# Attention step of a two-block kernel: the weighted sum in two groups a step, and one group of maxima moved by one turn

## The chip, the cores and the metric

The kernel runs on one core of one Trainium2 chip. The metric is the device time of one execution in microseconds (us). A core has five engines that run side by side and meet through semaphores: TensorE (PE in the profile, its weight loads PEld), VectorE (DVE), ScalarE (ACT), GpSimd (POOL) and the queue that issues transfers (SP).

## The reference

Two blocks follow each other: a chunked gated linear attention block, and a block with grouped-query attention beside a convolution. The change touches only the attention of the second block:

```python
# 8 query heads of 64, 2 key/value heads, 2048 queries, 256 context keys + 2048 keys = 2304 keys
s = jnp.einsum('bqkgd,bskd->bkgqs', qblk, k).astype(jnp.float32) * scale
pr = jax.nn.softmax(s, axis=-1).astype(v.dtype)
return jnp.einsum('bkgqs,bskd->bqkgd', pr, v)
```

## The kernel before, in words

The program has phases one after another: modulation, the first block, the projections, `attention`, `output`. `attention` walks over 32 steps (8 query heads times 4 blocks of 512 queries). In a step the 2304 keys are 18 tiles of 128, and each key tile is a turn `kt`, 0 to 17. A score tile (L1864, L1865) is two matmuls into one of three PSUM banks `bank_s`; ScalarE turns it into `p_f` by an exponential (L1928).

The exponential needs the negated maximum of each query's row. It is found a step ahead: for step i+1, 20 "pieces" (L1824), matmuls of 128 queries by 512 keys (every fifth by 256), go into four PSUM banks `bank_m`. VectorE reduces each to a column of maxima (L1960), then makes one column of the five (L1965) and negates it into `mz` (L1969). TensorE turns `mz` into a row with four transposes (`max_row`, L1831), and ScalarE copies the row (L1911) into the operand of the next step's scores. The pieces go in five groups of four, at the turns that `PIECES_OF_TURN` marks (2, 4, 9, 10, 14). `max_row(i+1)` stands at turn 15 and waits for `mz`. An even piece p waits until the pieces up to p-3 of its step have been reduced, because it and its neighbour take over banks that those held:

```python
if p % 2 == 0:
    need(pe, mx_read, i * NP + max(p - MBANKS + 2, 0))
```

The weighted sum `p_f` times `v` (L1839) is taken for pairs of key tiles, nine pairs a step, into one bank `bank_o` (`weigh`). `GROUP_AT` says at which turn which pairs stand: pairs 0 to 2 at turn 9, pairs 3 to 5 at turn 14, and pairs 6 to 8 at turn 2 of the next step. Within a turn TensorE's order is: the scores, the pieces of that turn, then the weighted sum of that turn.

The denominators are sums of `p_f` over the key tiles: GpSimd adds pairs 1 to 6 (L1809), VectorE adds pairs 7 and 8 (L1977) and folds (L1981). TensorE sums over partitions (`sum_den`, L1847, turn 5) and spreads the reciprocal (L1854, turn 7); VectorE adds and scales the output (L1985, L1990, L1996). Each engine executes its list strictly in the order written, and a wait at the head holds all that is behind it.

Of the kernel before, what the change touches and what calls it, by code (L numbers as in the profile page):

```python
# [1673 lines left out]
def attention(nc, d, keep):  # L1674
# [5 lines left out]
    POOL_ADDS = 6  # L1680
    DVE_ADDS = NPR - 1 - POOL_ADDS + 1
    SBANKS, MBANKS = 3, 4
    GROUP_AT = {2: (6, 7, 8), 9: (0, 1, 2), 14: (3, 4, 5)}
    GROUP_STEPS = (NQH // NKV) * NB
    STEPS = NKV * GROUP_STEPS
    PIECES = [(qt, n) for qt in range(NT) for n in range(-(-KEYS // TB))]
    NP = len(PIECES)

    PIECES_OF_TURN = [0, 0, 4, 0, 4, 0, 0, 0, 0, 4, 4, 0, 0, 0, 4, 0, 0, 0]
    TURN_PIECES = [list(range(sum(PIECES_OF_TURN[:kt]), sum(PIECES_OF_TURN[:kt + 1]))) for kt in range(NKT)]  # L1690
    assert sum(PIECES_OF_TURN) == NP
    with ExitStack() as ctx:
# [34 lines left out]
        def need(eng, semaphore, n):  # L1727

            if isinstance(n, int) and n <= 0:
                return  # L1730
            eng.wait_ge(semaphore, UP + n)
# [4 lines left out]
        def steps(eng, body):  # L1736


            last = GROUP_STEPS - 1
            for g in range(NKV):  # L1740
                base = g * GROUP_STEPS
                body(base, 0, g, g - 1 if g else None, g)
                body(base + 1, 1, g, g, g)
                with eng.Fori(1, GROUP_STEPS // 2 - 1) as it:
                    for s in range(2):
                        body(it * 2 + (base + s), s, g, g, g)
                body(base + last - 1, 0, g, g, g)
                body(base + last, 1, g, g, g + 1 if g + 1 < NKV else None)

        nc.all_engine_barrier()  # L1750
        with nc.Block() as block:
# [61 lines left out]
            def _(pe):  # L1813
                def piece(i, s, g, p):

                    qt, n = PIECES[p]
                    width = min(TB, KEYS - TB * n)
                    rows = slice(HD * (p % 2), HD * (p % 2 + 1))
                    if p == 0:
                        pe.wait_ge(q_hi_done, UP + i + 1)  # L1820
                        need(pe, row_read, i)
                    if p % 2 == 0:
                        need(pe, mx_read, i * NP + max(p - MBANKS + 2, 0))
                    pe.matmul(M[p % MBANKS][:, 0:width], q_c[s][rows, P * qt:P * (qt + 1)], k_a[g][rows, TB * n:TB * n + width],  # L1824
                              start=True, stop=True).then_inc(mx_done, 1)

                def max_row(i):

                    pe.wait_ge(mz_done, UP + i + 1)
                    for qt in range(NT):  # L1830
                        last = pe.transpose(M[0][0:HD + 1, P * qt:P * (qt + 1)], mz[:, qt, :], ident[:])  # L1831
                    last.then_inc(row_done, 1)

                def weigh(i, s, g, j):
                    pe.wait_ge(p_done, UP + i * NKT + 2 * j + 2)
                    if j == 0:
                        need(pe, o_done, i)
                    for half in range(2):
                        last = pe.matmul(O[HD * half:HD * (half + 1), :], v[g][:, 2 * j + half, :], p_f[:, 2 * j + half, :],  # L1839
                                         start=(j == 0), stop=(j == NPR - 1))  # L1840
                    last.then_inc(pv_done, 1)

                def sum_den(i, s):
                    pe.wait_ge(den_dve, UP + (i + 1) * DVE_ADDS)
                    pe.wait_ge(o_sum, UP + i + 1)
                    for qt in range(NT):
                        last = pe.matmul(O[:, qt:qt + 1], den[s][:, 0, P * qt:P * (qt + 1)], ones[:, 0:1], start=True, stop=True)  # L1847
                    last.then_inc(den_sum, 1)

                def spread_reciprocal(i):  # L1850

                    pe.wait_ge(recip_done, UP + i + 1)
                    for qt in range(NT):
                        last = pe.transpose(O[:, P * qt:P * (qt + 1)], recip[:, qt:qt + 1].broadcast_to([P, P]), ident[:])  # L1854
                    last.then_inc(r_row, 1)

                def body(i, s, g, before, after):
                    pe.wait_ge(row_read, UP + i + 1)
                    pe.wait_ge(q_lo_done, UP + i + 1)
                    pe.wait_ge(q_copied[s], UP + 32 * (i // 2) + 32)  # L1860
                    for kt in range(NKT):
                        need(pe, p_done, i * NKT + kt - SBANKS + 1)
                        keys = slice(P * kt, P * (kt + 1))
                        pe.matmul(S[kt % SBANKS][:], k_a[g][:, keys], q_a[s][:], start=True, stop=False)  # L1864
                        pe.matmul(S[kt % SBANKS][:], k_b[g][:, keys], q_b[s][:], start=False, stop=True).then_inc(s_done, 1)  # L1865
                        if after is not None:
                            for p in TURN_PIECES[kt]:
                                piece(i + 1, 1 - s, after, p)
                        if kt == 2 and before is not None:
                            for j in GROUP_AT[kt]:  # L1870
                                weigh(i - 1, 1 - s, before, j)
                        if kt in (9, 14):
                            for j in GROUP_AT[kt]:
                                weigh(i, s, g, j)
                        if kt == 5 and before is not None:
                            sum_den(i - 1, 1 - s)
                        if kt == 7 and before is not None:
                            spread_reciprocal(i - 1)
                        if kt == 15 and after is not None:
                            max_row(i + 1)  # L1880
# [7 lines left out]
                pe.wait_ge(v_landed, UP + 16 * NKV)  # L1888
                pe.wait_ge(ones_row, UP + NKV)
                steps(pe, body)  # L1890
                for j in GROUP_AT[2]:
                    weigh(STEPS - 1, 1, NKV - 1, j)
# [464 lines left out]


PHASES = [mixing_and_projections, attention, output]


# [65 lines left out]
```

## Time and profile before

| | |
|---|---|
| median of 3 runs | 2750.14 us (2749.21 to 2752.74) |
| the profiled execution | 2759.44 us, of which 2757.7 us are its span |
| TensorE busy | 2496.7 us, 91% |
| VectorE, ScalarE, GpSimd busy | 1734.0 us, 1014.8 us, 766.4 us |
| first and last weighted-sum matmul (attention) | 1707.5 us and 2442.2 us |

A row of the timeline gives the start in us from the span's start, the time that it took, the engine, the line, the operation with the tile that it writes and those that it reads, and how many instructions are merged in it; the square bracket is the idle time of that engine before it and who ended it.

### The profile page before, as it was taken

The page shows a single profiled execution, that of the slowest core. Times are in us where ns is not written, and L with a number is a line of the kernel's source. Part 1 is how long each engine was busy: PE and PEld are TensorE (multiplying, and loading weights), DVE is VectorE, ACT ScalarE, POOL GpSimd, SP SyncE. Part 2 cuts the span into 40 slices and gives each one's busy share as a digit, 9 for nine tenths or more (in the row PEclk, how much of TensorE's full clock was granted, in tenths as well). Part 3 has the DMA queues.
Part 4 walks back from the last instruction along what each step waited for, and adds up shares of the span by engine and source line. Part 5 has one row for each costly group of instructions (what it writes and reads, how often), then busy time and mean ns, then how long its engine had stood idle before and what let it go on. Part 6 is the DMA issues. An engine that isn't in the chain of part 4 may idle for free. (4 is left out here: it accounts for less than half of the span.)

```text
span 2757.7 us, 34578 instructions
## 1 busy us (share of the span) xinstructions
PE 2496.7 (91%) x11297; PEld 1715.5 (62%) x11297; DVE 1734.0 (63%) x2720; ACT 1014.8 (37%) x1768; POOL 766.4 (28%) x353
## 2 busy tenths in 40 slices
PE   3898899999999998999999985999999999956998
PEld 1576677777777776777677762444444544424776
DVE  2336563553546351779897984777777777746665
ACT  3234443434344341322222123444444444433222
POOL 0233311101111110113111013666666666532000
PEclk8899999999999999999999995999999999977999
DMA  6964887478467646578666644111111111133334
GB/s 238 328 221 138 265 283 256 141 252 328 161 225 266 248 148 246 183 256 314 206 231 223 221 150 106 28 29 29 29 29 29 29 29 29 25 119 130 129 127 154
DMA packets 224570, 453.46 MB, mean 164 GB/s; under 512 B 23285, under 2 KB 82027, under 8 KB 224196
## 3 DMA queue, kind: packets, MB, share of 16 engines
q1 hardware_dynamic: 193400, 351.07, 37.6%
q10 hardware_dynamic: 31052, 100.87, 10.5%
q8 instruction: 68, 1.11, 0.2%
q14 instruction: 50, 0.41, 0.0%
HBM read 328.89 MB, written 109.35 MB: 159 GB/s over the span
## 5 line engine op out<-in xcount | busy, mean ns | idle before, releaser
L527 PE MATMUL gla_bank_g<-mid_a_hi,mid_w_hi 128*128 128x512 f32 x1024 | 419.1, 409 | 23.7 <-DVE mid_a_lo L1049 10.4
L1960 DVE TENSOR_REDUCE att_mx<-att_bank_m 128x1 f32<-128x512 f32 (+1 forms) x640 | 365.6, 630 | 113.9 <-PE att_bank_m L1824 110.1
L1928 ACT ACTIVATE att_p_f<-att_bank_s 128x512 f32<-128x512 f32 x576 | 317.9, 598 | 290.1 <-PE att_bank_s L1865 283.9
L527 PE MATMUL gla_bank_g<-mid_a_lo,mid_w_hi 128*128 128x512 f32 x1024 | 405.6, 396 | 0.0
L527 PE MATMUL gla_bank_g<-mid_a_hi,mid_w_lo 128*128 128x512 f32 x1024 | 405.2, 396 | 0.0
L1809 POOL TENSOR_TENSOR att_den<-att_den,att_p_f 128x1024 f32<-128x1024 f32 x160 | 378.7, 2367 | 36.8 <-ACT att_p_f L1928 24.7
L1578 DVE SCALAR_TENSOR_TENSOR proj_conv_acc<-proj_conv_in,proj_conv_w,proj_conv_acc 128x512 f32<-128x512 f32 (+1 forms) x480 | 360.0, 818 | 0.0
L1839 PE MATMUL att_bank_o<-att_p_f,att_v 128*64 128x512 f32 x1152 | 270.4, 604 | 0.0
L1864 PE MATMUL att_bank_s<-att_q_a,att_k_a 128*128 128x512 f32 x576 | 258.7, 449 | 1.0 <-ACT att_q_b L1911 1.0
L527 PEld LDWEIGHTS gla_bank_g<-mid_a_hi,mid_w_hi 128*128 128x128 f32 x1024 | 196.6, 192 | 87.7 <-issue 29.9
L1865 PE MATMUL att_bank_s<-att_q_b,att_k_b 65*128 65x512 f32 x576 | 230.3, 400 | 0.0
L527 PEld LDWEIGHTS gla_bank_g<-mid_a_hi,mid_w_lo 128*128 128x128 f32 x1024 | 196.1, 191 | 42.9
L527 PEld LDWEIGHTS gla_bank_g<-mid_a_lo,mid_w_hi 128*128 128x128 f32 x1024 | 196.7, 192 | 40.8 <-issue 2.4
L1864 PEld LDWEIGHTS att_bank_s<-att_q_a,att_k_a 128*128 128x128 f32 x576 | 109.7, 190 | 137.2 <-issue 101.0
L473 POOL TENSOR_TENSOR mid_w_lo<-first_w_raw,mid_w_hi 128x1024 fp32r<-128x1024 f32 x22 | 55.6, 2529 | 404.0 <-ACT mid_w_hi L703 404.0
L1839 PEld LDWEIGHTS att_bank_o<-att_p_f,att_v 128*64 128x64 f32 x1152 | 74.6, 137 | 146.1 <-issue 96.5
L1388 PE MATMUL proj_bank_g<-mid_a_hi,mid_w_hi 128*128 128x512 f32 x352 | 142.3, 404 | 13.8 <-PEq L1210 9.3
L1824 PE MATMUL att_bank_m<-att_k_a,att_q_c 64*128 64x512 f32 (+1 forms) x640 | 122.2, 434 | 34.4 <-ACT att_k_a L1900 31.4
L1809 POOL TENSOR_TENSOR att_den<-att_p_f 128x1024 f32<-128x1024 f32 x32 | 75.8, 2370 | 258.7 <-ACT att_p_f L1928 258.7
L1307 POOL TENSOR_TENSOR proj_qraw<-proj_qraw,proj_cos 128x512 f32<-128x512 f32 x20 | 33.6, 1678 | 402.0 <-DMA proj_qsin<-proj_qraw 402.0
L1388 PE MATMUL proj_bank_g<-proj_u_hi,mid_w_hi 128*128 128x512 f32 x352 | 141.5, 402 | 0.0
L1388 PE MATMUL proj_bank_g<-proj_u_lo,mid_w_hi 128*128 128x512 f32 x352 | 138.8, 394 | 0.0
(359 smaller groups left out, 4328.8 us busy)
## 6 DMA issues: line engine op xcount, KB each, us to landing
mid_w_hi<-scratch_w_hi SPq DMA_DIRECT2D x100, 512.0 KB, 4.2
mid_w_lo<-scratch_w_lo SPq DMA_DIRECT2D x100, 512.0 KB, 5.6
mid_w_hi<-scratch_w_hi ACTq DMA_DIRECT2D x84, 512.0 KB, 3.8
mid_w_lo<-scratch_w_lo ACTq DMA_DIRECT2D x84, 512.0 KB, 5.0
scratch_w_hi<-mid_w_hi SPq DMA_DIRECT2D x54, 512.0 KB, 6.1
scratch_w_lo<-mid_w_lo SPq DMA_DIRECT2D x54, 512.0 KB, 6.9
mod_wslab<-in_ada_w SPq DMA_DIRECT2D x6, 2048.0 KB, 17.9
first_w_raw<-in_gla_w_in SPq DMA_DIRECT2D x24, 512.0 KB, 5.9
```

The source lines that it names most:

```text
L473: pool.tensor_tensor(w2_lo[:], w_raw[m % 2][:], w2_hi[:].bitcast(F32), ALU.subtract).then_inc(w2_rest, 1)
L527: last = pe.matmul(banks[s % 2][:], w[:, k, :], a[:, k, :], start=(k == 0 and n == 0), stop=(k == KT - 1 and n == 2))
L1307: pool.tensor_tensor(qraw[:, i, :], qraw[:, i, :], cos[:], ALU.mult).then_inc(q_cos, 1)
L1388: last = pe.matmul(G[j % 2][:], w[:, k, :], a[half][:, k, :], start=(k == 0 and n == 0), stop=(k == KT - 1 and n == 2))
L1578: dve.scalar_tensor_tensor(acc, src, conv_w[:, c, k:k + 1], acc, ALU.mult, ALU.add).then_inc(taps, 1)
L1809: pool.tensor_tensor(den[s][:], pair(0) if j == 1 else den[s][:], pair(j), ALU.add).then_inc(den_pool, 1)
L1824: pe.matmul(M[p % MBANKS][:, 0:width], q_c[s][rows, P * qt:P * (qt + 1)], k_a[g][rows, TB * n:TB * n + width], start=True, stop=True).then ...
L1839: last = pe.matmul(O[HD * half:HD * (half + 1), :], v[g][:, 2 * j + half, :], p_f[:, 2 * j + half, :], start=(j == 0), stop=(j == NPR - 1))
L1864: pe.matmul(S[kt % SBANKS][:], k_a[g][:, keys], q_a[s][:], start=True, stop=False)
L1865: pe.matmul(S[kt % SBANKS][:], k_b[g][:, keys], q_b[s][:], start=False, stop=True).then_inc(s_done, 1)
L1928: act.activation(p_f[:, kt, :], S[kt % SBANKS][:], ACT.Exp, scale=float(HD) ** -0.5).then_inc(p_done, 1)
L1960: dve.reduce_max(mx[:, qt, n:n + 1], M[p % MBANKS][:, 0:min(TB, KEYS - TB * n)], AX_X).then_inc(mx_read, 1)
```

## The change

Of the three groups of the weighted sum two remain: pairs 5 to 8 at turn 2 of the next step and pairs 0 to 4 at turn 11. Turns 9 and 14 have none. The pieces 12 to 15 move from turn 10 to turn 11, so that they stand in front of the group of five. Turns 9 and 14 keep their pieces (8 to 11 and 16 to 19). No instruction is added or taken away.

```diff
-    GROUP_AT = {2: (6, 7, 8), 9: (0, 1, 2), 14: (3, 4, 5)}
+    GROUP_AT = {2: (5, 6, 7, 8), 11: (0, 1, 2, 3, 4)}
-    PIECES_OF_TURN = [0, 0, 4, 0, 4, 0, 0, 0, 0, 4, 4, 0, 0, 0, 4, 0, 0, 0]
+    PIECES_OF_TURN = [0, 0, 4, 0, 4, 0, 0, 0, 0, 4, 0, 4, 0, 0, 4, 0, 0, 0]
-                        if kt in (9, 14):
+                        if kt == 11:
                             for j in GROUP_AT[kt]:
                                 weigh(i, s, g, j)
```

## Rows read from the trace of the kernel before

**Rows 1.** The page, busy time of each engine, share of the span and instructions
```profile
PE 2496.7 (91%) x11297; PEld 1715.5 (62%) x11297; DVE 1734.0 (63%) x2720; ACT 1014.8 (37%) x1768; POOL 766.4 (28%) x353
```

**Rows 2.** Windows, attention: length, busy us (instructions) by engine, granted clock, DMA share, GB/s
```profile
1711.60:2440.80 729.20, 722.69 (x3372) 361.93 (x3370) 553.54 (x886) 361.24 (x658) 444.11 (x188) 1.00 0.11 27
```

**Rows 3.** Waits, 1710 to 2440 us: engine and line, waited for, us in total, times, longest
```profile
ACT att_p_f L1928 <- PE att_bank_s L1865: 277.2, 186, 6.0
...
PE att_bank_m L1831 <- DVE att_mz L1969: 6.5, 31, 0.2
```

**Rows 4.** Timeline of TensorE's matmuls over one step
```profile
2002.95 0.73 PE L1824 MATMUL att_bank_m<-att_k_a,att_q_c 64*128 64x512 f32 x4
...
2006.34 0.50 PE L1864 MATMUL att_bank_s<-att_q_a,att_k_a 128*128 128x512 f32 x1
...
2007.48 0.72 PE L1824 MATMUL att_bank_m<-att_k_a,att_q_c 64*128 64x256 f32 x4
...
2012.00 0.73 PE L1824 MATMUL att_bank_m<-att_k_a,att_q_c 64*128 64x512 f32 x4
...
2016.05 0.73 PE L1824 MATMUL att_bank_m<-att_k_a,att_q_c 64*128 64x512 f32 x4
2016.71 0.50 PE L1864 MATMUL att_bank_s<-att_q_a,att_k_a 128*128 128x512 f32 x1
...
2018.80 0.73 PE L1824 MATMUL att_bank_m<-att_k_a,att_q_c 64*128 64x512 f32 x4
...
2022.18 0.50 PE L1864 MATMUL att_bank_s<-att_q_a,att_k_a 128*128 128x512 f32 x1
2022.52 0.39 PE L1865 MATMUL att_bank_s<-att_q_b,att_k_b 65*128 65x512 f32 x1
2023.12 0.65 PE L1831 MATMUL att_bank_m<-ident_sb,att_mz 128*65 128x128 f32 x4 [0.21 <-DVE att_mz L1969]
...
2026.25 0.51 PE L1824 MATMUL att_bank_m<-att_k_a,att_q_c 64*128 64x512 f32 x2
```

**Rows 5.** Timeline of TensorE's weight loads inside the weighted sum of turn 2
```profile
2004.52 0.14 PEld L1839 LDWEIGHTS att_bank_o<-att_p_f,att_v 128*64 128x64 f32 x2 [0.28 <-issue]
2004.95 0.14 PEld L1839 LDWEIGHTS att_bank_o<-att_p_f,att_v 128*64 128x64 f32 x2 [0.28 <-issue]
```

**Rows 6.** Timeline of VectorE in the same step
```profile
2012.53 2.22 DVE L1960 TENSOR_REDUCE att_mx<-att_bank_m 128x1 f32<-128x512 f32 x4 [0.58 <-PE att_bank_m L1824]
...
2019.33 2.22 DVE L1960 TENSOR_REDUCE att_mx<-att_bank_m 128x1 f32<-128x512 f32 x4 [0.53 <-PE att_bank_m L1824]
...
2021.79 1.27 DVE L1969 TENSOR_SCALAR att_mz<-att_m 128x4 f32<-128x4 f32 x1
```

**Rows 7.** Timeline of GpSimd in the same step
```profile
2007.79 2.37 POOL L1809 TENSOR_TENSOR att_den<-att_p_f 128x1024 f32<-128x1024 f32 x1 [8.07 <-ACT att_p_f L1928]
2010.23 7.28 POOL L1809 TENSOR_TENSOR att_den<-att_den,att_p_f 128x1024 f32<-128x1024 f32 x3
2018.24 4.80 POOL L1809 TENSOR_TENSOR att_den<-att_den,att_p_f 128x1024 f32<-128x1024 f32 x2 [0.73 <-ACT att_p_f L1928]
```

**Rows 8.** Timeline ahead of the first step, where only the 20 pieces run
```profile
1680.96 11.12 DVE L1960 TENSOR_REDUCE att_mx<-att_bank_m 128x1 f32<-128x512 f32 x20 [7.56 <-PE att_bank_m L1824]
...
1692.32 0.17 DVE L1969 TENSOR_SCALAR att_mz<-att_m 128x4 f32<-128x4 f32 x1
```

**Rows 9.** Timeline of TensorE's matmuls in the first block, two gaps
```profile
544.86 0.47 PE L527 MATMUL gla_bank_g<-mid_a_hi,mid_w_hi 128*128 128x512 f32 x1 [2.10 <-DVE mid_a_lo L1049]
...
788.71 0.47 PE L527 MATMUL gla_bank_g<-mid_a_hi,mid_w_hi 128*128 128x512 f32 x1 [2.10 <-DVE mid_a_lo L1049]
```

**Rows 10.** Windows behind three such gaps, columns as in Rows 2
```profile
544.90:548.30 3.40, 3.16 (x13) 2.30 (x14) 3.40 (x7) 3.40 (x7) 0.00 (x0) 1.00 0.96 349
...
790.10:793.40 3.30, 3.30 (x9) 2.53 (x9) 3.30 (x6) 2.24 (x4) 0.98 (x1) 0.50 1.01 323
...
1221.50:1224.90 3.40, 3.40 (x15) 2.63 (x15) 3.40 (x5) 0.00 (x0) 1.74 (x1) 1.00 0.87 300
```

## The prediction

> **What bounds the kernel now.** I read the page first, for the share of each engine: TensorE is busy for 91% of the span, no other engine for more than 63% [rows 1]. The windows narrow this to the stage of the change: in 729.2 us of attention TensorE is busy for 722.7 us at a granted clock of 1.00, VectorE for 76% of it, GpSimd for 61%, ScalarE for 50% [rows 2]. The waits say who waits for whom: ScalarE waits for scores (277 us in total), and TensorE's matmuls have one wait of their own, 31 times up to 0.2 us, for `mz` [rows 3]. So attention is TensorE's list of instructions laid end to end, and time is won or lost only in that list. Then the timeline of one step, to learn the price of each item and how far each wait is from biting. From the pieces of turn 2 at 2002.95 to those of the next step at 2026.25 it is 23.30 us [rows 4].
>
> **Prices, from the timeline.** Four pieces until the next instruction: 0.66 us (2016.05 to 2016.71). A group of pieces followed by three pairs: 3.39 us (2002.95 to 2006.34), so three pairs cost 2.73 us. Inside a group the weight loads follow each other by 0.43 us, two of these slots to a pair [rows 5], so a pair costs 0.86 us and three 2.58 us; the other 0.15 us is what a group costs for being one. From the first score matmul to the following pieces two scores take 1.14 us (2006.34 to 2007.48) and four 2.09 us (2016.71 to 2018.80), so three take about 1.61 us.
>
> **The gain.** The pairs are as many as before. One group fewer is 0.15 us a step, and nothing else in TensorE's list gets shorter: all three groups stand behind pieces today and both groups do afterwards, and a switch from pieces to scores costs the same 0.66 us as one to the weighted sum. Over 32 steps this is 4.8 us.
>
> **The first loss, turn 11.** Pieces 14 and 15 need banks that pieces 10 and 11 hold until VectorE has reduced them. Today the group of three stands between turn 9's pieces (2012.00) and turn 10's (2016.05), while the four reductions end at 2012.53 + 2.22 = 2014.75 [rows 4, 6], 1.3 us early. Afterwards only two scores stand between: the pieces of turn 11 come 0.66 + 1.14 = 1.80 us behind those of turn 9, and their second half at 1.80 + 0.33 = 2.13 us. The fourth reduction ends at 2.75 us, and about 0.05 us passes until TensorE goes on. A wait of 2.80 - 2.13 = 0.67 us. Everything behind it in TensorE's list waits too, the five pairs first.
>
> **The second loss, turn 15.** `max_row` needs all 20 reductions, the column, and `mz`. Behind the pieces of turn 14 (2018.80) today come the group of three, the score of turn 15 and then the row at 2023.12, 4.32 us later. Of these, 0.21 us is already a wait for `mz`. The chain on VectorE is: first reduction 0.53 us behind the pieces, 2.22 us for the four, `mz` begun at 2021.79, 2.99 us behind the pieces [rows 6]. Here `mz` took 1.27 us, but 0.17 us ahead of the first step, where GpSimd does nothing [rows 8]; and it ended at 2023.06, when GpSimd's last addition ended (2018.24 + 4.80 = 2023.04) [rows 7]. So GpSimd's addition holds it up by 1.10 us. Afterwards the group of three is gone from turn 14, and the row comes at best 2.99 + 0.17 + 0.06 = 3.22 us behind the pieces, while TensorE is done with the score of turn 15 at about 0.66 + 0.34 + 0.3 = 1.3 us (2022.18 to 2022.52 for the half score). It stands for about 1.9 us, where today it stands for a few tenths. Behind it are the scores of turns 16 and 17; ScalarE catches up meanwhile and its exponentials are not late afterwards.
>
> **Is `mz` still held?** GpSimd's first addition needs the exponential of turn 3, which comes 0.86 us later because the group at turn 2 has four pairs. Additions take 2.44 us each (2007.79 to 2010.23) [rows 7]. Counted from the pieces of turn 2, the first starts at 4.84 + 0.86 = 5.70 us and five are over at 17.9 us. The sixth needs the exponential of turn 13. That score stands behind the group of five: pieces of turn 9 at 9.05 + 0.86 = 9.91, second half of turn 11's at 12.71, group from 13.04, its end 0.15 + 5 x 0.86 = 4.44 later at 17.48, score 13 at about 18.3, its exponential about 19.5. So the sixth addition runs from 19.6 to 22.0 us. The pieces of turn 14 stand at 17.48 + 1.61 = 19.09 us and `mz` wants to start at 22.08. It just misses the addition, so I count 0.17 us. The Trainium skill (SBUF — State Buffer, Who interferes with whom) says that a VectorE `tensor_scalar` and a GpSimd instruction exclude each other from a shared pair of ports for a whole instruction; the trace agrees (1.27 against 0.17 us), and if the two still met as they do today, that page would have the row 1.10 us later and the total 34 us higher.
>
> **The sum of a step**, from pieces of turn 2 to pieces of turn 2:
> - turn 2 to turn 9: 9.05 + 0.86 = 9.91 us
> - turn 9 to turn 14: 2.80 + 0.33 + 4.44 + 1.61 = 9.18 us (today 6.80)
> - turn 14 to the row: 3.22 us (today 4.32)
> - row to turn 2: 3.13 us, unchanged
> - together 25.44 us against 23.30: 2.14 us more
>
> Steps with pieces and a row: 31 of 32. 31 x 2.14 = 66.3 us. In the last step GpSimd starts 0.86 us later and its sum bounds the tail, so 0.9 us more. Together +67 us: against the profiled execution (2759.44 us) 2826.6 us, and against the median of the runs, which lies 9.3 us lower, 2817 us.
>
> **The clock.** A TensorE that stands for 1.8 to 1.9 us in each step may lose its full clock. Today attention has 1.00 from 1711.6 us on. In the first block and the projections the trace has 6 gaps of 2.05 to 2.22 us. After three of them the granted clock fell to 0.50 (1.2 GHz) for 3.4 us, after three it did not; two equal gaps of 2.10 us show both [rows 9, 10]. Of 11 gaps of 1.58 to 1.79 us one was followed by a fall, and gaps of about 3 us and more nearly always were. The new gap is 1.8 us, but what follows is only four small transposes for 0.4 us, so it lies between these classes. A fall costs 1.3 to 1.7 us: in 3.3 us at 0.50 nine matmuls ran, in 3.4 us at 1.00 fifteen, and at half clock nothing more than half can be lost [rows 10]. I take 1.5 us and a fall in half of the steps: 16 x 1.5 = 24 us, 2841 us. The bounds are none (2817) and all 31 (2817 + 47 = 2864). The Trainium skill (TensorE: Matmul & The Clock Gate, HAM oscillation) describes a kernel whose array waits in every tile and is throttled again each time; by that rule it would be the upper end, 2864 us.
>
> **The rivals.**
> - The two waits as worked out, clock at 1.00 throughout: 2817 us. For it: ten of 11 gaps under 1.8 us did nothing. 0.25.
> - The two waits, clock in half of the steps (forecast): 2841 us. 0.38.
> - The clock falls in nearly every step: 2864 us. For it: the gap and the transposes together are 2.2 us, and the steps repeat alike. 0.25.
> - `mz` is still held by GpSimd, because the sixth addition starts later than I count: 1.10 us more in 31 steps, 2851 us without the clock. For it: it misses by 0.1 us only. If it starts later still, at the same time as `mz`, it is up to 2.4 us. 0.08.
> - Not slower: the waits don't appear, and 0.15 us a step is left, 2745 us. It decides if the chain from the pieces of turn 14 to `mz` fits under 1.3 us; it measures 3.2 us with nothing in its way, and nothing in the diff makes a reduction shorter. What could save it is that TensorE has slack elsewhere to give back, but it is busy for 722.7 of 729.2 us. 0.04, split between faster and same.
>
> The likeliest by itself spans 2828 to 2855 us. The range of 8 in 10 takes in both clock bounds with a few us for the prices: 2811 to 2870. The measurement can tell about 0.2% (5.5 us) from no change; the chance of slower by more is 0.96.
>
> **What the next profile would show.** Right: in the waits `bank_m` L1831 for `mz` rises to about 1.8 us times 31 and L1824 for `mx` to about 0.7 us times 31; `mz` takes 0.17 us; a step is at least 25.4 us; the stage takes 66 us more, the rest nothing. Wrong in the clock: PEclk in attention stays 1.00, or falls in every step. Wrong in the hold: `mz` takes over 1 us. What would overthrow it all is a row that comes right behind the score of turn 15.

## The result: slower, by more than was forecast

The changed kernel takes 2884.86 us in the median (2878.56 to 2894.05), against 2751.44 us of the kernel before on the same chip. The ratio is 1.0458, with an interval of 1.0437 to 1.0478. The forecast had the sign and both waits; its 2841 us and its upper bound of 2870 us were too low. The profiled execution of the changed kernel took 2894.05 us, with a span of 2892.3 us.

First the waits of TensorE's matmuls (PE) and weight loads (PEld) on VectorE in the profile after, from 1720 to 2560 us (engine and line, waited for, us in total, times, longest), which answer to [rows 3]:

```profile
PEld att_bank_m L1831 <- DVE att_mz L1969: 70.2, 31, 2.3
...
PE att_bank_m L1831 <- DVE att_mz L1969: 56.6, 31, 1.9
...
PEld att_bank_m L1824 <- DVE att_mx L1960: 36.3, 61, 0.8
...
PE att_bank_m L1824 <- DVE att_mx L1960: 15.0, 30, 0.5
```

The wait for `mz` was 6.5 us in total before and is 56.6 us now, 31 times up to 1.9 us. The reader should take the times and the longest from such a line: 31 is once a step. The line of `mx` reads 0.5 us, 30 times, where the prediction wrote about 0.7: it counts only the time in which the matmuls stood idle. Then the timeline of TensorE's matmuls over one step, which answers to [rows 4]:

```profile
2037.73 0.73 PE L1824 MATMUL att_bank_m<-att_k_a,att_q_c 64*128 64x512 f32 x4
2038.39 3.65 PE L1839 MATMUL att_bank_o<-att_p_f,att_v 128*64 128x512 f32 x16
...
2047.63 0.73 PE L1824 MATMUL att_bank_m<-att_k_a,att_q_c 64*128 64x512 f32 x4
...
2049.43 0.50 PE L1824 MATMUL att_bank_m<-att_k_a,att_q_c 64*128 64x512 f32 x2
2050.43 0.51 PE L1824 MATMUL att_bank_m<-att_k_a,att_q_c 64*128 64x256 f32 x2 [0.50 <-DVE att_mx L1960]
2050.86 4.51 PE L1839 MATMUL att_bank_o<-att_p_f,att_v 128*64 128x512 f32 x20
...
2056.91 0.73 PE L1824 MATMUL att_bank_m<-att_k_a,att_q_c 64*128 64x512 f32 x4
...
2060.12 0.65 PE L1831 MATMUL att_bank_m<-ident_sb,att_mz 128*65 128x128 f32 x4 [1.82 <-DVE att_mz L1969]
...
2061.12 0.63 PE L1864 MATMUL att_bank_s<-att_q_a,att_k_a 128*128 128x512 f32 x1
...
2064.59 0.73 PE L1824 MATMUL att_bank_m<-att_k_a,att_q_c 64*128 64x512 f32 x4
```

Counted from 2037.73: pieces of turn 9 at 9.90 us (worked out: 9.91), second half of turn 11's at 12.70 (12.71), pieces of turn 14 at 19.18 (19.09), row at 22.39 (22.3). Each station is within 0.1 us of where the prediction put it. What it had only in half of the steps stands in the last two lines: from 2061.12 on a score matmul takes 0.63 us where it took 0.40 to 0.50, and the step ends at 26.86 us instead of 25.44. The windows around that place and the next ones (length, busy us and instructions of TensorE, its loads, VectorE, ScalarE, GpSimd, then the granted clock) show why, as [rows 2, 10] do for before:

```profile
2037.10:2061.00 23.90, 21.57 (x103) 10.81 (x102) 15.28 (x28) 9.94 (x19) 14.18 (x6) 1.00 0.10 25
2061.00:2064.40 3.40, 3.40 (x10) 2.31 (x8) 2.44 (x4) 2.68 (x5) 0.00 (x0) 0.51 0.28 64
...
2088.30:2095.20 6.90, 6.90 (x20) 3.30 (x20) 5.09 (x7) 2.87 (x5) 0.00 (x0) 0.51 0.28 77
```

The granted clock falls to 0.50 (1.2 GHz) behind the row. "The row" is from here on the four transposes of `max_row`, and a fall is a stretch at 0.50. For 31 rows the clock record of attention has 30 falls, 22 of 3.4 us and 8 of 6.8 us; only the first row, in the stretch at 0.50 with which the stage begins, has none of its own. Steps with a short fall take 26.84 us in the mean, those with a long one 28.60 us, all together 27.32 us.

VectorE and GpSimd at the same place, which answer to [rows 6, 7]:

```profile
2057.47 2.35 POOL L1809 TENSOR_TENSOR att_den<-att_den,att_p_f 128x1024 f32<-128x1024 f32 x1 [1.91 <-ACT att_p_f L1928]
...
2059.90 0.17 DVE L1969 TENSOR_SCALAR att_mz<-att_m 128x4 f32<-128x4 f32 x1
```

GpSimd's addition ends at 2059.82, and `mz` starts at 2059.90 and takes 0.17 us: it just misses the addition, by 0.08 us.

Attention, from its first to its last instruction, took 782.8 us before and 904.7 us after, 121.9 us more. The first block (1008.4 to 1016.3 us) and the projections (573.4 to 578.2 us) took 13 us more in this profile, though nothing in them changed. Over the profiles of this study they lie between 1006.6 and 1016.6 us and between 566.3 and 578.2 us in no order that follows the kernel, so I take that as scatter, with the changed kernel near the upper end of both. I compare kernels by their step and by attention's length, and by ratios on one chip.

Attention begins while the clock is at 0.50 in every profile (until 1711.6 us in the kernel before), which I call the slow start, and its first step takes from 22.25 to 27.27 us in an order that doesn't follow the kernel: 25.62 us before, 27.16 us in the changed kernel. Lengths of attention compare only to a few us for that. Closer is the steady step, the mean over the steps behind the first that have no fall: 23.32 us before.

### The profile page after: what moved, and what is told of

The parts are those of the page before. It is cut to its first block and busy times, and to the rows that moved or that the text cites. A ratio compares the mean times of both kernels' runs of the same rounds, so it can differ in the third digit from the quotient of the medians.

```text
span 2892.3 us, 34590 instructions
## 1 busy us (share of the span) xinstructions
PE 2569.6 (89%) x11297; PEld 1772.0 (61%) x11297; DVE 1693.4 (59%) x2720; ACT 1022.2 (35%) x1768; POOL 762.7 (26%) x353
## 3 DMA queue, kind: packets, MB, share of 16 engines
q8 instruction: 68, 1.11, 0.2%
## 5 line engine op out<-in xcount | busy, mean ns | idle before, releaser
L1960 DVE TENSOR_REDUCE att_mx<-att_bank_m 128x1 f32<-128x512 f32 (+1 forms) x640 | 362.5, 628 | 200.8 <-PE att_bank_m L1824 197.0
L1864 PE MATMUL att_bank_s<-att_q_a,att_k_a 128*128 128x512 f32 x576 | 281.8, 489 | 1.0 <-ACT att_q_b L1911 1.0
L1865 PE MATMUL att_bank_s<-att_q_b,att_k_b 65*128 65x512 f32 x576 | 255.8, 444 | 0.0
L1864 PEld LDWEIGHTS att_bank_s<-att_q_a,att_k_a 128*128 128x128 f32 x576 | 125.4, 218 | 110.7 <-issue 57.1
L1824 PE MATMUL att_bank_m<-att_k_a,att_q_c 64*128 64x512 f32 (+1 forms) x640 | 134.7, 460 | 47.7 <-ACT att_k_a L1900 29.6
L1388 PE MATMUL proj_bank_g<-proj_u_hi,mid_w_lo 128*128 128x512 f32 x352 | 140.3, 398 | 0.0
```

Of the source, the lines that this page charges most:

```text
L1388: last = pe.matmul(G[j % 2][:], w[:, k, :], a[half][:, k, :], start=(k == 0 and n == 0), stop=(k == KT - 1 and n == 2))
L1960: dve.reduce_max(mx[:, qt, n:n + 1], M[p % MBANKS][:, 0:min(TB, KEYS - TB * n)], AX_X).then_inc(mx_read, 1)
```

## The experiments

Three theories were open. **Clock**: the two waits cost what was worked out, and the rest is the clock, which falls because TensorE stands before the row. **Waits**: the waits cost more than worked out and the clock only follows. **Pace**: falls begin 27.3 us apart and hold the steps to that, whatever is saved. A step is the time between the pieces of turn 2 of two steps, its mean is over 30 steps. The ratio is taken on the chip that ran the kernel; the kernel before took 2751.44 us on that of the changed kernel, and 2757.73, 2756.99 and 2762.20 us on the three others. The falls are those behind the slow start.

| kernel | median us | ratio to before, interval | attention us | step us | falls for 31 rows (of 3.4, 6.8, 10.2 us) |
|---|---|---|---|---|---|
| before | 2751.44 | | 782.8 | 23.40 | 0 |
| changed | 2884.86 | 1.0458 (1.0437 to 1.0478) | 904.7 | 27.32 | 22, 8, 0 |
| 8 matmuls in the gap | 2829.69 | 1.0251 (1.0226 to 1.0275) | 851.1 | 25.58 | 0 |
| 3 in the gap | 2824.60 | 1.0238 (1.0213 to 1.0263) | 849.2 | 25.52 | 0 |
| 2 in the gap | 2833.63 | 1.0265 (1.0228 to 1.0303) | 853.2 | 25.65 | 1, 0, 0 |
| 1 in the gap | 2867.77 | 1.0389 (1.0351 to 1.0427) | 890.5 | 26.85 | 15, 2, 3 |
| group of five at turn 14 | 2767.70 | 1.0038 (1.0018 to 1.0059) | 790.1 | 23.65 | 0 |
| pieces at turn 8 | 2876.39 | 1.0409 (1.0379 to 1.0439) | 899.9 | 27.13 | 15, 14, 0 |
| the same, 3 in the gap | 2817.26 | 1.0202 (1.0168 to 1.0236) | 837.7 | 25.15 | 0 |
| group of 14 to turn 2 | 2891.74 | 1.0493 (1.0469 to 1.0516) | 915.8 | 27.64 | 25, 3, 3 |
| pieces alone | 2762.44 | 1.0011 (0.9995 to 1.0027) | 782.7 | 23.43 | 0 |
| groups alone | 2932.53 | 1.0645 (1.0625 to 1.0666) | 954.1 | 28.90 | 15, 1, 14 |
| the same, 3 in the gap | 2891.53 | 1.0475 (1.0434 to 1.0516) | 906.2 | 27.35 | 21, 1, 0 |
| two groups, all covered | 2761.21 | 1.0014 (0.9998 to 1.0029) | 782.2 | 23.37 | 0 |

The diffs below are against the changed kernel, where nothing else is said.

### Work in the gap

```diff
                         if kt == 15 and after is not None:
+                            need(pe, p_done, i * NKT + 14)
+                            for _ in range(8):
+                                pe.matmul(S[16 % SBANKS][:], k_a[g][:, keys], q_a[s][:], start=True, stop=True)
                             max_row(i + 1)
```

> The changed kernel, and at turn 15, ahead of max_row, eight extra score matmuls (about 0.21 us each, 1.7 us together) into the bank that turn 16 overwrites anyway; their results are not used. They fill the stretch of 1.8 us in which TensorE stands for mz. Theory (the two waits cost 2.14 us a step and the rest of the loss is the clock, which falls because TensorE stands before the row): granted clock 1.00 through attention, a step of 25.4 us, about 2820 us, faster than the changed kernel in spite of more work. Rival 1 (the loss beyond 2.14 us comes from the waits themselves, the clock only follows): no faster than 2885 us. Rival 2 (the matmuls don't fit in the gap and simply add): 2885 + 31 x 1.7 = 2938 us.

The added `need` holds the extra matmuls until ScalarE has emptied the bank that they write. With three instead of eight:

> The same with three extra matmuls (0.64 us), so that TensorE stands for about 1.2 us before the row instead of 1.8. No gap of 1.2 us in the trace of before was followed by a fall of the clock. Theory: no falls or few, 2818 to 2835 us. Rival (any standing before the light transposes of the row brings the clock down): as the changed kernel, 2885 us.

Both are faster than the changed kernel, with more work in TensorE's list. The timeline of the run with eight, TensorE's matmuls of one step from the pieces of turn 14 on, and the window over its attention (the added lines shift L1969 to L1972 and L1960 to L1963 in this run and the others with extra matmuls):

```profile
2053.32 0.73 PE L1824 MATMUL att_bank_m<-att_k_a,att_q_c 64*128 64x512 f32 x4
2054.55 2.00 PE L1882 MATMUL att_bank_s<-att_q_a,att_k_a 128*128 128x512 f32 x8
2056.53 0.65 PE L1831 MATMUL att_bank_m<-ident_sb,att_mz 128*65 128x128 f32 x4
```

```profile
1711.60:2500.00 788.40, 773.28 (x3572) 410.81 (x3571) 516.18 (x887) 355.01 (x646) 435.54 (x185) 1.00 0.10 25
```

The row comes 3.21 us behind the pieces, as it does without the eight: VectorE's chain sets it. The clock stays at 1.00. Attention is 53.6 us shorter than in the changed kernel (55.5 us with three), and 68.3 and 66.4 us longer than before, where the prediction had 67 us for the two waits. A steady step is 25.56 us in both (25.44 worked out). This rules out the theory of the waits: they cost what was worked out to within 0.12 us a step, and all else in attention is the clock.

### How long TensorE may stand

> Two extra score matmuls (0.43 us) ahead of the row, so that TensorE stands 1.4 us. Three extra ones left no fall. If falls go over gradually with the length of the gap: some falls here, 2830 to 2860 us; if they stop at once: none, 2822 us.

> One extra score matmul (0.21 us) ahead of the row, so that TensorE stands 1.6 us. In the trace of before one of 11 gaps of 1.58 to 1.79 us was followed by a fall. If the length of the gap decides: falls in few steps, under 2840 us. If the low work around the gap (the light transposes behind it) decides with it: falls in most steps, 2860 to 2885 us.

The waits of the runs with three, two and one matmul, from 1710 to 2440 us, which leaves out the last rows:

```profile
PE att_bank_m L1831 <- DVE att_mz L1972: 32.3, 29, 1.2
```

```profile
PE att_bank_m L1831 <- DVE att_mz L1972: 38.0, 28, 1.4
```

```profile
PE att_bank_m L1831 <- DVE att_mz L1972: 42.8, 27, 1.7
```

The last number is the longest, which is one row; the total by the times gives what a row has. With three matmuls in the gap TensorE stands 1.11 us and no fall comes, with two 1.35 us and one fall comes for 31 rows, with one 1.58 us and 20 come, with none 1.82 us and 30. So it goes over gradually, and most of it between 1.35 and 1.82 us. Both times lie in a forecast range, 2833.63 us in that of a gradual change and 2867.77 us in that of falls in most steps. Each matmul shortens the standing and is work in its place at once; no run separates the two. The window of the run with one:

```profile
1711.60:2530.00 818.40, 754.16 (x3318) 394.78 (x3315) 513.61 (x882) 355.98 (x639) 431.37 (x183) 0.94 0.10 24
```

In [rows 9, 10] two equal gaps of 2.10 us had different ends, and ten of 11 gaps of 1.58 to 1.79 us did nothing. Here 1.58 us sufficed 20 times in 31. The light transposes behind the gap can't be the whole reason: four of those gaps, of 1.62 to 1.65 us, have eight transposes behind them and brought no fall. No run took the transposes away, so what makes this gap worse than those stays open. What the runs show is that the share found at single gaps elsewhere, one in 11, did not hold for this one, 20 in 31.

### The group back in front of the row

```diff
-    GROUP_AT = {2: (5, 6, 7, 8), 11: (0, 1, 2, 3, 4)}
+    GROUP_AT = {2: (5, 6, 7, 8), 14: (0, 1, 2, 3, 4)}
-                        if kt == 11:
+                        if kt == 14:
```

> The changed kernel with the group of five at turn 14 instead of turn 11; the pieces stay at turn 11. Theory: the group covers the reductions ahead of the row again, the clock stays at 1.00, the wait of 0.67 us at turn 11 stays, the group saved gives 0.15 us and the 0.29 us that the row waited before are covered too: a step of 23.5 us, 2758 us. Rival (the loss is at turn 11 or in having two large groups): well above 2800 us.

A steady step is 23.70 us, 0.2 us over what was worked out and 0.38 us over before. Attention is 7.3 us longer than before, with a first step that was 3.4 us shorter. Two large groups do no harm, and the wait of turn 11, which is still there, brings no fall. The timeline shows it, and behind it that the row has no wait any more (no bracket):

```profile
2044.58 0.50 PE L1824 MATMUL att_bank_m<-att_k_a,att_q_c 64*128 64x256 f32 x2 [0.50 <-DVE att_mx L1960]
...
2047.28 4.51 PE L1839 MATMUL att_bank_o<-att_p_f,att_v 128*64 128x512 f32 x20
...
2052.29 0.60 PE L1831 MATMUL att_bank_m<-ident_sb,att_mz 128*65 128x128 f32 x4
```

### Less waiting at turn 11, with and without falls

```diff
-    PIECES_OF_TURN = [0, 0, 4, 0, 4, 0, 0, 0, 0, 4, 0, 4, 0, 0, 4, 0, 0, 0]
+    PIECES_OF_TURN = [0, 0, 4, 0, 4, 0, 0, 0, 4, 0, 0, 4, 0, 0, 4, 0, 0, 0]
```

> The changed kernel with pieces 8 to 11 at turn 8 instead of 9, so that three scores stand ahead of turn 11's pieces and their wait shrinks from 0.67 to about 0.2 us. Theory by single costs: 31 x 0.47 = 15 us less, 2870 us. Rival: the falls of the clock in the profile of the changed kernel begin 27.3 us apart, and the steps, of 26.9 and 28.6 us, have just that mean; if the falls set the pace, what is saved at turn 11 is paid back in longer falls and the time stays at 2885 us.

The mean step shrank by 0.19 us and not by 0.47. The single steps tell more than the mean: most of them alternate between 26.36 us (a short fall) and 28.25 us (a fall of 6.8 us). Each is 0.35 to 0.5 us shorter than its kind in the changed kernel, but there are 14 long falls where there were 8. In that alternation the mean is 27.3 us, just that of the changed kernel (27.3 us without its first step): where every row had its fall the clock took back all of the saving, as the theory of the pace has it. The 0.19 us come from the places where it didn't, above all one row without a fall, whose step took 25.03 us. The wait at turn 11 has shrunk to 0.02 us here and the falls still come, 29 for 31 rows. Then the same with three matmuls in the gap:

> The run with pieces 8 to 11 at turn 8, and three extra score matmuls ahead of the row as before. With falls of the clock the 0.47 us saved at turn 11 brought 0.19 us a step in the mean (27.13 against 27.32). Theory (the price of a wait adds up only while the clock stands, and the falls took the saving back): no falls, a step of 25.55 - 0.47 = 25.08 us, the full 0.47 us against the run with three extra matmuls, about 2810 us. Rival (the wait at turn 11 was not worth 0.47 us in the first place): 25.3 us or more.

No falls, 25.09 us in a steady step against 25.56: the full 0.47 us. The wait at turn 11 was priced rightly.

### The row alone

Against the kernel before:

```diff
-    GROUP_AT = {2: (6, 7, 8), 9: (0, 1, 2), 14: (3, 4, 5)}
+    GROUP_AT = {2: (3, 4, 5, 6, 7, 8), 9: (0, 1, 2)}
-                        if kt in (9, 14):
+                        if kt == 9:
```

> The kernel before with the group of turn 14 moved to turn 2 of the next step (pairs 3 to 8 there, pairs 0 to 2 at turn 9), pieces as before (turns 2, 4, 9, 10, 14). So the row of turn 15 has lost its cover, and turn 10 keeps its own. Without the clock a step would be 25.2 us (mz begins while GpSimd's last addition runs and is held for some 0.5 us). Theory with falls priced singly at 1.3 us: 26.5 us, about 100 us over before. Theory of the pace (once TensorE's standing brings the clock down in each step, steps take 27.3 us in the mean, whatever is saved): about 120 us over before, as the changed kernel. Rival (the wait at turn 11 is part of what brings the clock down): no falls here, 60 us over before.

The falls come without any wait at turns 9 to 11, so the standing before the row is enough, though it is longer here than in the changed kernel. The attention is 133 us longer than before, more than either number. The timeline gives the reason for the size:

```profile
2046.47 4.78 POOL L1809 TENSOR_TENSOR att_den<-att_den,att_p_f 128x1024 f32<-128x1024 f32 x2 [0.73 <-ACT att_p_f L1928]
2047.03 0.73 PE L1824 MATMUL att_bank_m<-att_k_a,att_q_c 64*128 64x512 f32 x4
2050.02 1.26 DVE L1969 TENSOR_SCALAR att_mz<-att_m 128x4 f32<-128x4 f32 x1
...
2051.34 0.65 PE L1831 MATMUL att_bank_m<-ident_sb,att_mz 128*65 128x128 f32 x4 [2.92 <-DVE att_mz L1969]
```

TensorE stands for 2.92 us: `mz` is held until GpSimd's last addition ends at 2051.25, by 1.09 us, twice the 0.5 us that I had counted. The row comes 4.31 us behind the pieces, which puts the step without falls at 18.43 + 4.31 + 3.16 = 25.90 us (pieces of turn 2 to those of turn 14, to the row, and from the row on as in the run with three matmuls). The steps of 27.2 us, 23 of the 30, are 1.3 us above it, a short fall each. So near to 27.3 us they don't decide between single costs and the pace.

### The groups alone, and the pieces alone

```diff
-    PIECES_OF_TURN = [0, 0, 4, 0, 4, 0, 0, 0, 0, 4, 0, 4, 0, 0, 4, 0, 0, 0]
+    PIECES_OF_TURN = [0, 0, 4, 0, 4, 0, 0, 0, 0, 4, 4, 0, 0, 0, 4, 0, 0, 0]
```

> The changed groups (pairs 5 to 8 at turn 2, pairs 0 to 4 at turn 11) with pieces 12 to 15 left at turn 10. Only one score stands between turn 9's and turn 10's pieces, so TensorE waits about 0.67 us a step longer than in the changed kernel. Theory by single costs: 31 x 0.67 = 21 us over the changed kernel, 145 us over before. Theory of the pace: a step stays at 27.3 us, with fewer of the long falls, and the time is that of the changed kernel, 120 to 133 us over before.

Both were wrong: a step of 28.90 us is 1.6 us over the changed kernel's, where single costs gave 0.67 us and the pace none. A pace of 27.3 us whatever is saved or added is refuted; from the fourth step on the steps alternate between 28.4 and 29.65 us. The falls are longer, as a window behind one row shows:

```profile
2068.10:2078.30 10.20, 9.84 (x26) 5.39 (x28) 6.59 (x10) 3.57 (x6) 0.07 (x1) 0.50 0.19 51
```

The next run says what the step is without the gap before the row:

> The changed groups with pieces 12 to 15 left at turn 10, and three extra score matmuls ahead of the row. It gives the step without falls: theory 25.55 + 0.67 = 26.22 us (about 2845 us), which would put 2.7 us a step of that kernel's 28.9 us on the clock. Rival (the move from turn 10 to 11 is worth more than the wait): 27 us or more.

Steps without a fall take 26.14 to 26.25 us, the 26.22 that was expected. But the clock still falls 22 times, and the time is 2891.53 us instead of 2845. One fall comes close behind the slow start; the 21 others begin at another place than before, 12.7 to 14.1 us behind the pieces of turn 2. The timeline there shows it:

```profile
2066.91 0.49 PE L1824 MATMUL att_bank_m<-att_k_a,att_q_c 64*128 64x512 f32 x2 [0.22 <-DVE att_mx L1963]
2068.11 0.79 PE L1824 MATMUL att_bank_m<-att_k_a,att_q_c 64*128 64x256 f32 x2 [0.70 <-DVE att_mx L1963]
...
2069.98 6.97 PE L1839 MATMUL att_bank_o<-att_p_f,att_v 128*64 128x512 f32 x20
```

Two short waits with two light matmuls between them, 0.9 us in all, and the group of five behind them runs for 6.97 us instead of 4.51. With the pieces at turn 11 the wait is a single one of 0.50 us in these lines, and there no fall comes. Whether the second wait or its length brings them wasn't tried. So the second line of the diff, the pieces' move, saves 0.67 us of waiting a step here, and more by the clock.

The pieces' move without the groups', the kernel before with pieces 12 to 15 at turn 11:

> The kernel before with its three groups, and only pieces 12 to 15 moved from turn 10 to turn 11. The group of turn 9 covers turn 11; the pieces of turn 14 follow three scores behind those of turn 11, so that their second half waits about 0.2 us. A step of 23.5 us, 6 us over before, clock 1.00. Rival (the move of the pieces alone carries the loss of turn 11): 20 us over before.

A steady step of 23.38 us against 23.32, some 2 us in 31 steps where I had 6, and attention within 0.1 us of before; its clock is 1.00. The pieces of turn 14 do wait, so that their second half comes 0.2 us later, but `mz` then meets less of GpSimd's addition (0.68 us in the median instead of 1.27), which gives most of it back. The ratio of 1.0011 can't be told from no change.

### Two groups with every reduction covered

```diff
-    GROUP_AT = {2: (5, 6, 7, 8), 11: (0, 1, 2, 3, 4)}
+    GROUP_AT = {2: (5, 6, 7, 8), 14: (0, 1, 2, 3, 4)}
-    PIECES_OF_TURN = [0, 0, 4, 0, 4, 0, 0, 0, 0, 4, 0, 4, 0, 0, 4, 0, 0, 0]
+    PIECES_OF_TURN = [0, 0, 4, 0, 4, 0, 0, 0, 4, 0, 0, 4, 0, 0, 4, 0, 0, 0]
-                        if kt == 11:
+                        if kt == 14:
```

> Two groups without an uncovered reduction: pairs 5 to 8 at turn 2, pairs 0 to 4 at turn 14 in front of the row, pieces at turns 2, 4, 8, 11, 14. Against the run with the group at turn 14 (23.70 us a step) the wait at turn 11 shrinks by 0.47 us: 23.23 us a step against 23.32 before, 3 us faster than before, clock 1.00. Rival (GpSimd or the exponentials become late with two large groups): a step over 23.5 us.

The steady step is 23.25 us (23.23 worked out), against 23.32. Attention takes 782.2 us against 782.8, with a first step 1.3 us longer. The ratio, 1.0014 (0.9998 to 1.0029), shows no gain and leaves out the 3 us that I had forecast. So two groups can be had at no cost that is clear of noise, and what the steps save, some 2 us by the trace, doesn't show in the kernel's time.

## Why the prediction was right in kind and wrong in size

- **What bounds attention** was right: TensorE's list. Matmuls put into its gap cost nothing, each wait put into it shows in full as long as the clock stays up.
- **The gain**, 0.15 us a step for one group fewer, was rightly called small. The run with everything covered is 0.07 us a step shorter than before, with 0.2 us of wait left at turn 11; the 0.15 us by itself was not measured.
- **The first loss**, 0.67 us at turn 11, was right: the second half of the pieces comes 1.00 us behind the first instead of 0.33, and 0.47 us of it came back when the pieces moved to turn 8 with the clock steady.
- **The second loss**, the row 3.22 us behind the pieces of turn 14, was right: 3.21 us.
- **The hold by GpSimd** was right by a hair: `mz` took 0.17 us. It started 0.08 us behind the end of the addition, and both came 0.1 us later than worked out, so luck had its part. The Trainium skill (SBUF — State Buffer, Who interferes with whom) has a `tensor_scalar` in a mode with two ports and a GpSimd instruction exclude each other for a whole instruction; the runs agree, with 1.27 us before, 0.17 us after, and 1.26 us again in the run whose group of turn 14 moved to turn 2.
- **The sum without the clock**, 67 us, was right: 66.4 and 68.3 us in the two runs without falls.
- **The clock** is the step that failed: "I take 1.5 us and a fall in half of the steps: 16 x 1.5 = 24 us". For 31 rows there were 30 falls, and 8 of them were twice as long as the 3.4 us of the rows that I had. Measured against 25.56 us, a step with a short fall costs 1.28 us more and one with a long fall 3.04 us. Of the 30 steps 21 are short and 8 long: 26.9 + 24.3 = 51.2 us. With an estimated 1.3 us for the fall behind the last row it is some 52 us, where I had 24. I had the case of a fall in nearly every step as a rival, and mis-sized it too, at 47 us, because I let no fall be longer than 3.4 us, though the trace of before has one of 6.8 us at 435.1 us, by a gap of 3.02 us. The Trainium skill (TensorE: Matmul & The Clock Gate, HAM oscillation) has the picture, a wait in every tile with a new throttling each time, but its waits are of 3 to 5 us. Here 1.82 us brought the same, so the picture came true and its lengths did not. The prediction named the picture without these lengths; by them it was no ground for the upper end.
- The remainder: 67 and 52 us make 119 us, attention measured 121.9. The steady step is 0.12 us longer than the 25.44 us of the sum, which is 3 to 4 us. With 52 us in the place of 24 the same sum would have given 2869 us, at the upper end of the range. The medians differ by 133 us. In the profiled executions the surplus over attention lies in stages that the change does not touch (13 us); of the others no profile says where it lies.

Left open: what decides whether a fall lasts 3.4, 6.8 or 10.2 us. My idea that steps settle at 27.3 us held when 0.47 us was saved and was refuted by steps of 28.9 us when a wait was added. In these kernels with falls a price per step can't be added up: 0.47 us saved gave 0.19 us, and 0.67 us of waiting more cost 1.6 us.

## What to carry to other kernels

A group of matmuls that looks like plain work may be the cover of a dependent chain on another engine. Before moving it, measure the chain from its first input to the waiting instruction (here 3.2 us) and lay it beside what is left in between (here 1.3 us). And if TensorE is to stand at the same place in every step, price the clock apart from the wait and for every step: here it cost 52 us beside 67 us. A quick test tells the two apart, a few matmuls without use put into the gap; if the kernel gets faster with them, as here by 60 us with three, the clock had a part in it.

## What the runs showed of the hardware that was not expected

- Standing 1.11 us before the row left the clock at 1.00 in all steps, 1.35 us brought one fall for 31 rows, 1.58 us 20, and 1.82 us 30. Elsewhere ten of 11 gaps of 1.58 to 1.79 us brought none.
- Behind two waits of 0.22 and 0.70 us around two light matmuls the clock came down 21 times in 31 steps; behind one wait of 0.50 us at the same place in none.
- Falls lasted 3.4, 6.8 or 10.2 us. One of 6.8 us, from 2088.3 to 2095.2 us, reaches into the group of four at turn 2, where TensorE has no wait at all.
